# Scores issued in pairs on the two row halves of TensorE, and a third score place in the differential attention

## What is computed

```python
# differential: q, k [S, 8 heads, 2 maps, 64], v [S, 8 heads, 128]
s = einsum('bqhmd,bkhmd->bmhqk', qb, k) + bias      # two maps a head
p = softmax(where(allowed, s, NEG_INF))
a = p[:, 0] - lam_full * p[:, 1]
o = einsum('bhqk,bkhe->bqhe', a, v)
# chunked: q, k, v [S, 16 heads, 64]
s = einsum('bqhd,bkhd->bhqk', qc, kband) + bias
o = einsum('bhqk,bkhd->bqhd', softmax(s), vband)
```

## Time and profile before

| | |
|---|---|
| median of three runs | 1262.27 us |
| profiled execution | 1263.72 us |
| its span | 1261.8 us |
| granted TensorE clock over the span | 0.972 |
| TensorE busy | 1141.0 us, 90% |
| VectorE busy | 606.7 us, 48% |
| ScalarE busy | 441.7 us, 35% |
| DMA | 354.23 MB, mean 281 GB/s |

### The profile page before, as it was taken

The page is one execution under the profiler, slowest core; times in us unless marked ns, Lnnn a source line. Parts: engine busy times, 40 slices in busy tenths (PEclk is TensorE's granted clock), DMA queues, the critical chain, the costliest instruction groups (busy, mean ns, idle before and its releaser), DMA issues.

```text
span 1261.8 us, 16821 instructions
## 1 busy us (share of the span) xinstructions
PE 1141.0 (90%) x6516; PEld 765.5 (61%) x6516; DVE 606.7 (48%) x1170; ACT 441.7 (35%) x770; POOL 69.1 (5%) x137
## 2 busy tenths in 40 slices
PE   5999979888999997996799999987999999999986
PEld 4677547578999995875563443323787863443422
DVE  3268456446666666647642323224773542323223
ACT  5344512236444556536340110103654640110200
POOL 2111232100000000000000000000000000000000
PEclk9899989988999999998899999999999999999999
DMA  9998897635677772573079999997576279999995
GB/s 292 361 290 264 298 351 265 240 117 165 180 229 227 221 226 70 198 266 134 34 304 405 412 413 414 414 414 301 189 244 256 71 275 413 412 412 414 414 413 209
DMA packets 162955, 354.23 MB, mean 281 GB/s; under 512 B 9912, under 2 KB 78776, under 8 KB 162752
## 3 DMA queue, kind: packets, MB, share of 16 engines
q1 hardware_dynamic: 146864, 296.04, 64.2%
q0 software_dynamic: 16000, 57.16, 12.9%
q10 hardware_dynamic: 16, 0.02, 0.0%
HBM read 352.12 MB, written 7.36 MB: 285 GB/s over the span
## 4 chain that ended last, share of the span: by engine, by line
PE 72%; DMA 14%; DVE 9%; ACT 3%; issue 1%; POOL 0%; SPq 0%; ACTq 0%; DVEq 0%
PE bank L534 35%; PE bank L1066 12%; DMA ering<-in_moe_w_up 9%; PE bank L1077 8%; DMA ering<-in_ada_w 3%; PE bank L481 3%; PE bank L1034 3%; DMA wraw<-in_w_in 2%; PE bank L683 1%; PE bank L816 1%; DVE wlo L524 1%; PE bank L1723 1%; PE bank L1715 1%; PE bank L1726 1%; PE bank L1138 1%
## 5 line engine op out<-in xcount | busy, mean ns | idle before, releaser
L524 DVE TENSOR_TENSOR wlo<-wraw,whi 128x1024 fp32r<-128x1024 f32 x150 | 179.6, 1222 | 73.9 <-ACT whi L520 71.7
L520 ACT ACTIVATE whi<-wraw 128x1024 fp32r<-128x1024 f32 x150 | 153.9, 1054 | 75.2 <-PE bank L534 54.1
L534 PE MATMUL bank<-a_hi,whi 128*128 128x256 f32 x512 | 148.7, 290 | 3.2 <-DVE wlo L524 2.1
L534 PE MATMUL bank<-a_lo,whi 128*128 128x256 f32 x512 | 146.5, 286 | 0.0
L534 PE MATMUL bank<-a_hi,wlo 128*128 128x256 f32 x512 | 146.4, 286 | 0.0
L1066 PE MATMUL bank<-ering,work 128*64 128x512 f32 x592 | 134.3, 596 | 11.9 <-DMA ering<-in_moe_w_up 10.5
L534 PEld LDWEIGHTS bank<-a_hi,whi 128*128 128x128 f32 x512 | 99.9, 195 | 17.6 <-issue 15.6
L1267 DVE TENSOR_TENSOR work<-work,bank 128x512 f32<-128x512 f32 x16 | 11.0, 687 | 206.4 <-PE bank L1066 206.4
L534 PE MATMUL bank<-whi,a_hi 128*128 128x512 f32 x256 | 102.1, 399 | 2.7 <-DVE a_lo L737 2.7
L1066 PEld LDWEIGHTS bank<-ering,work 128*64 128x64 f32 x592 | 41.1, 137 | 102.7 <-issue 78.7
L1175 ACT ACTIVATE o_hi<-work 128x512 fp32r<-128x512 f32 x32 | 20.2, 630 | 236.0 <-DVE work L1235 235.5
(11 more groups left out here) (305 smaller groups left out, 1869.8 us busy)
## 6 DMA issues: line engine op xcount, KB each, us to landing
ering<-in_moe_w_down SPq DMA_DIRECT2D x44, 1024.0 KB, 18.3
ering<-in_moe_w_up SPq DMA_DIRECT2D x42, 1024.0 KB, 18.2
ering<-in_ada_w POOLq DMA_DIRECT2D x80, 512.0 KB, 6.0
ering<-in_moe_w_gate SPq DMA_DIRECT2D x32, 1024.0 KB, 18.2
work<-in_moe_w_gate SPq DMA_DIRECT2D x16, 1024.0 KB, 16.5
wraw<-in_w_in SPq DMA_DIRECT2D x28, 512.0 KB, 8.1
wraw<-in_a_w_qkv SPq DMA_DIRECT2D x24, 512.0 KB, 4.7
work<-in_moe_w_down SPq DMA_DIRECT2D x12, 1024.0 KB, 18.4
```

The source lines that it names most:

```text
L520: nc.scalar.activation(w_hi(c), wraw[:, c % RING, :], ACT.Copy).then_inc(w_hi_done, 1)
L524: nc.vector.tensor_tensor(w_lo(u[0]), wraw[:, u[0] % RING, :], w_hi(u[0]).bitcast(F32), ALU.subtract).then_inc(w_lo_done, 1)
L534: mm = nc.tensor.matmul(out_ap, l, r, start=first and n == 0, stop=last and n == len(terms) - 1)
```

## The change

`scores` takes one or two map numbers. It first waits for the banks of all of them, then issues the 128-column matmuls of all, then the 256-column matmuls of all, so that with two maps the row halves take turns. In phase 0 it is called with one head, as before. In phase 1 it is called with the two maps of a head. In phase 2 it is called with two heads in every even step: heads i + 2 and i + 3 in step i, where before each step i had head i + 3. Heads 0 and 1 are issued ahead of the loop (before: 0, 1 and 2).

The differential attention gets a third score place for each head: `att_depth` returns ns = 3 for phase 1, `b2_sc` has 6 places instead of 4 and starts at 1024 instead of 2048 in the work tile, and the negated maxima (M_NM) move to the end of a `sm` tile that is 16 columns wider.

```diff
-        sm = sb("sm", [P, 640])
+        sm = sb("sm", [P, 656])
...
-        b2_sc = wk(2048, 4, 384)
+        b2_sc = wk(1024, 6, 384)
...
-        M_MX, M_NM, M_DEN, M_RD = 176, 184, 192, 208
+        M_MX, M_NM, M_DEN, M_RD = 176, 640, 192, 208
...
-            return 2 if ph == 0 else 4 // ATT[ph][1], 4 if ph == 2 else 2
+            return 2 if ph == 0 else 4 // ATT[ph][1], (2, 3, 4)[ph]
...
-            def scores(i):
-                for m in range(maps):
-                    n = i * maps + m
-                    bank = score_bank(ph, i, m)
-                    if i >= nb:
+
+            def scores(*ns_):
+                for n in ns_:
+                    if n >= nb * maps:
 
                         pe.wait_ge(sc_read, m0 + n + 1 - nb * maps)
-                    at = (n % 2) * 64
-                    q, k = q_of(n), k_of(n)
-                    nc.tensor.matmul(bank[:, 0:P], q[at:at + 64, 0:P], k[at:at + 64, 0:P], start=True, stop=True)
-                    nc.tensor.matmul(bank[:, P:P + S], q[at:at + 64, P:S], k[at:at + 64, :], start=True,
-                                     stop=True).then_inc(sc_ps, 1)
-
-
-            for i in range(nb - 1):
-                scores(i)
+                for t in range(T):
+                    for n in ns_:
+                        bank = score_bank(ph, n // maps, n % maps)
+                        at = (n % 2) * 64
+                        q, k = q_of(n)[at:at + 64, t * P:(t + 1) * P], k_of(n)[at:at + 64, 0:(t + 1) * P]
+                        mm = nc.tensor.matmul(bank[:, t * P:t * P + (t + 1) * P], q, k, start=True, stop=True)
+                        if t == 1:
+                            mm.then_inc(sc_ps, 1)
+
+            if ph == 0:
+                scores(0)
+            else:
+                scores(0, 1)
             for i in range(units + 2):
                 if before is not None:
                     before(i)
-                if i + nb - 1 < units:
-                    scores(i + nb - 1)
+                if ph == 0 and i + 1 < units:
+                    scores(i + 1)
+                if ph == 1 and i + 1 < units:
+                    scores(2 * i + 2, 2 * i + 3)
+                if ph == 2 and i % 2 == 0 and i + 2 < units:
+                    scores(i + 2, i + 3)
```

## The result

The changed kernel takes 1255.66 us (median of 18 runs, 1252.65 to 1259.03) against 1262.09 for the kernel before (18 runs, 1256.21 to 1265.22): a ratio of 0.9951, 95% interval 0.9940 to 0.9962, so 6.2 us less (4.8 to 7.6). Its profiled execution took 1255.53 us, with a span of 1253.7.

What follows compares the result with a forecast made beforehand. TensorE carries 72% of the chain; VectorE limits the differential stage, TensorE the chunked one. Gains of 4.5 us chunked and 3.2 us differential, 7.7 us off 1262.27, give 1254.6 us, range 1250.5 to 1259.6.

Steps and rivals of the forecast that it cites:

- TensorE's chunked step: Chunked attention: two TensorE steps fall from 3.89 to 2.97 us, five times, so 4.5 us less.
- What would be late next there: Chunked attention: ScalarE needs 1.24 us a head, VectorE 1.14, against TensorE's 1.48, so both fit.
- Alternation at zero: Score matmuls: alternating the row halves gains nothing by itself; bounds 0 and 0.3 us for each differential pair.
- The third place: Differential attention: six VectorE stalls for transposes, 3.6 us, go; 3.2 us gained after late scores, bounds 2.0 to 3.6.
- Does it reach the end: Expert stages behind the attentions: their stream starts after the attention and shifts whole, so all 7.7 us arrive.
- the column M_NM moves in `sm`, which costs nothing: Dilated attention step: moving the column costs zero, as the operations keep their shapes.
- expert stages of the old length: Expert stages: keeping their length was named as a sign that the prediction was right.
- only one stage: Rival: only the differential stage gains, 1259.1 us (chance 0.10), or only the chunked one, 1257.8 us (0.08).
- absorbed: Rival: expert streams end when they did, or the change doesn't do what it says; 1262 us, chance 0.07.
- slower: Rival: TensorE's clock falls to 1.2 GHz in the chunked stage, up to 1281 us; chance 0.05.
- the clock helps too: Rival: the low-clock stretch ending the differential stage goes in part, 1.3 to 2.7 us more, 1252 to 1253.3; chance 0.10.

Runs made afterwards that it cites:

- pairs only: The changed kernel with two score places instead of three in the differential attention; 1259.78 us, 0.9978 of the kernel before.
- pairs twice: The changed kernel with every pair of scores of the chunked attention issued twice; 1260.14 us, 0.9984 of the kernel before.
- no alternation: The changed kernel with both matmuls of one head before those of the other, still as a pair; 1255.93 us, 0.9946 of the kernel before.
- delay: The changed kernel with one VectorE multiplication in the norm behind the differential attention made three times; 1262.8 us, 0.9999 of the kernel before.
- clock kept: The changed kernel with unneeded matmuls in TensorE's pauses in and behind the differential attention; 1253.53 us, 0.9933 of the kernel before.

## Why the prediction was right, and where it was not

The time was 1255.66 us where 1254.6 was forecast, within its range; 6.2 us were gained where 7.7 were forecast. Point by point:

- **TensorE's chunked step**: two steps of 2.97 us instead of 3.89. Measured 2.90. The pair was 0.86 (0.87 forecast, from the earlier trace rows); the rest is that the second head's transposes took 0.33 instead of 0.38. Over five periods that is the difference between 4.5 and the 4.9 us measured. The mechanism and its size are confirmed by the stage of "pairs only" (25.49 us) and by "pairs twice"; at the end "pairs only" is 2.8 us below before, and 4.8 below the kernel that has the same shift.
- **What would be late next there**: nothing, as said. In the changed kernel ScalarE has 22.79 us of work from 954 to 980 us, TensorE 23.80, at the full clock. One wait stands at the start:

```profile
957.64 0.55 PE L823 MATMUL bank<-con,work 128*128 128x128 f32 x3 [1.38 <-ACT work L857]
```

 It is the wait for the first softmax, in which head 4's scores lay before. The rule of the Trainium skill's "TensorEngine Tiling (Array Packing)", section "PSUM Bottleneck", did not come to bear: ScalarE kept the pace of one head in 1.45 us.
- **Alternation at zero**: confirmed by "no alternation", with 0.86 to 0.87 us for a pair in both orders. By the strict program order that "TensorE: Matmul & The Clock Gate" of the Trainium skill gives in "The mechanism" (Part 3), the old order would by an estimate from the earlier trace rows cost some 0.3 us more for each pair; neither the stage (25.53 against 25.49) nor the pair shows it.
- **The third place**: the walk through the differential stage gave head 3 at 576.1, head 4 at 579.6 and head 7 at 588.9, 8.0, 11.5 and 20.8 us behind the first score at 568.06. Measured are 7.8, 11.7 and 20.7 (574.05, 577.98 and 586.99 less 566.27). The one wait for scores stood where it was forecast, at head 4, and was 0.85 us where 0.4 was forecast, with head 3 a little earlier; the period was 3.00. The stage is 3.3 us shorter (3.2). The tail kept its form: the last scaling starts 8.23 us behind head 7, and 8.24 before (600.32 less 592.08).
- **Does it reach the end**: yes, as said. "Pairs twice" and "delay" put time in before each stream, and it arrived, within 0.9 us.
- **The step that failed**: "the column M_NM moves in `sm`, which costs nothing". I costed the operations that use the column and not the tile that had to grow for it. A wider `sm` shifts `work` by 64 bytes, `work` holds three of the fifteen places of the expert stream, and the expert stages end on that stream. Costed at nothing, it measured 2.2 us in means (3.9 by the estimate at equal clocks), against the 2.0 between the 8.2 gained in the stages and the 6.2 at the end. It also broke the last thing that I named as a sign, "expert stages of the old length". That the forecast of the time came near is in part luck: the chunked gain, 0.4 us larger, made up for a part, and the shift's price happened to be small beside the range.

Of the rivals, "only one stage" falls by the changed kernel's own stages (28.94 and 25.49 us); "absorbed" by "delay" and "pairs twice"; "slower" by the clock of 1.00 in the chunked stage; "the clock helps too" did not happen in the changed kernel (0.62 and 0.82 in its differential stage), and the two kernels with the clock kept show what it would have been worth. Busy time by stretches of the changed kernel, to be held against the earlier trace rows:

```profile
571.00:580.00 9.00, 8.04 (x45) 5.98 (x45) 7.73 (x44) 6.46 (x27) 0.00 (x0) 0.62 0.69 277
580.00:594.00 14.00, 9.89 (x67) 8.34 (x64) 11.19 (x54) 9.92 (x37) 0.00 (x0) 0.82 0.00 1
954.00:980.00 26.00, 23.80 (x208) 20.44 (x208) 17.54 (x111) 22.79 (x83) 0.00 (x0) 1.00 0.63 244
```

## What to carry to other kernels

Where a stage waits on a place, walk it with the durations of its own rows, low-clock ones included, and ask what is late next: here that gave the differential stage's gain to 0.1 us. Put work on different row halves next to each other in TensorE's queue; the order within the pair is free. And when a tile must grow, look at every tile that is laid out behind it: a large stream's destination that moves by 64 bytes can cost as much as a small gain brings, and it shows as a rate, in stages that the diff does not touch.

## What the hardware showed that I had not expected

- **The position in SBUF that a load is written to changes its rate**: 413 GB/s with the three places in `work` where they were, 409 with them 64 or 128 bytes further. The mean duration of a packet of 4096 bytes from 700 to 830 us is 162.2 and 162.3 ns in the two profiles of before, and 163.6 to 163.7 in the others; it is 159 around the loads into `work` of before and 164 elsewhere. Section "How a descriptor splits into AXI transactions" of the Trainium skill's page "DMA: Bandwidth & Descriptors" says that a transaction that reads must start from a 256-byte boundary, and that for data which begin off one the bytes before them are fetched too and cost time. Here it is the place of writing that moved. A price of the position within 256 bytes would agree in kind; no run shows the transactions, nor which of the positions is the boundary.
- **A low clock outlasts its pause**, so the length of a stage depends on what TensorE does in pauses that cost nothing by themselves: the low stretch that begins behind the differential attention, at 599.2 us in the changed kernel, lasts 10.2 us. It covers the sixteen matmul records of line 683, which start at 604.03 us after 8.85 us without work and take 3.68 us there and 1.91 in "clock kept". With "clock kept" the differential stage ran at 1.00 and took 2.8 us less.
- **Most of the spread between runs of one kernel goes with the clock**: over all kernels, each about its own mean, the runs' times and their mean granted clocks correlate with −0.83, at 0.8 us for 0.001. The differential stage differs by 0.9 us between two profiles of the kernel before (32.26 and 31.37 us), which is why one stage length of one profile says less than the sums over 30 runs.
